# Per-column sums of the conditioning vectors: four transposes and four ScalarE copies with sums, where there were four products with a column of ones

## The reference, cut to what matters

```
c_act = silu(c)                               # one row of 1024
for i in range(4):
    mod = c_act @ ada_w[i] + ada_b[i]         # ada_w[i]: 1024 x 6144
    sh1, sc1, g1, sh2, sc2, g2 = split(mod, 6)
    h = modulate(rmsnorm(x, gain), sh1, sc1)  # h * (1 + sc1) + sh1
    x = x + g1 * mixer(h)                     # swa, gla, fox, swa in turn
    h = modulate(rmsnorm(x, gain), sh2, sc2)
    x = x + g2 * ((silu(h @ wg) * (h @ wu)) @ w_down)
```

## Time and profile before

| | |
|---|---|
| median of 3 runs | 2258.88 us (2257.32 to 2260.17) |
| the profiled execution's own time | 2258.98 us |
| its span, first to last instruction | 2257.2 us |
| mean granted PE clock | 0.989 |
| instructions | 33992 |
| DMA packets | 475.60 MB, mean 211 GB/s |

### The profile page before, as it was taken

One profiled execution on the slowest core, in us unless ns is written; L12 is line 12 of the kernel. 1 busy time (PEld: TensorE's weight loads), 2 busy tenths in 40 slices (PEclk: granted clock), 3 DMA queues, 4 the chain that ended last, 5 costly groups with the idle time before them and its releaser, 6 DMA issues.

```text
span 2257.2 us, 33992 instructions
## 1 busy us (share of the span) xinstructions
PE 2161.0 (96%) x13827; PEld 1925.4 (85%) x13827; DVE 1565.2 (69%) x2153; ACT 1029.4 (46%) x1698; POOL 186.2 (8%) x202
## 2 busy tenths in 40 slices
PE   6899999999999999989999999999999999999997
PEld 5799888888998888767999787899898899778996
DVE  5477757766777577566898677899745896657444
ACT  5344445544444455455444444433445434464333
POOL 1000001101000011011001001001000001111000
PEclk9999999999999999999999999999999999999999
DMA  8876745566766445623899534699643697525651
GB/s 281 285 227 229 254 156 165 172 224 225 240 232 233 157 160 173 229 98 126 283 342 346 180 119 143 223 350 356 220 145 131 236 353 242 177 85 177 201 188 66
DMA packets 297104, 475.60 MB, mean 211 GB/s; under 512 B 19936, under 2 KB 151466, under 8 KB 296948
## 3 DMA queue, kind: packets, MB, share of 16 engines
q1 hardware_dynamic: 286548, 440.67, 57.5%
q0 software_dynamic: 10400, 32.76, 4.8%
HBM read 465.88 MB, written 7.47 MB: 210 GB/s over the span
## 4 chain that ended last, share of the span: by engine, by line
PE 87%; DVE 6%; DMA 2%; ACT 2%; issue 2%; POOL 1%; SPq 0%; DVEq 0%; POOLq 0%; ACTq 0%
PE G L138 68%; PE A L138 16%; PE G L141 2%; DVE pool L158 1%; DMA raw<-in_w_in 1%; DVE wlo L150 1%; DVE pool L150 1%; ACT pool L144 1%; POOL sm L150 1%; PE A L141 1%; DVE X L150 1%; ACT HTh L144 0%; DVE sm L155 0%; DMA pool<-mod_rows 0%; DMA pool<-in_ada_b 0%
## 5 line engine op out<-in xcount | busy, mean ns | idle before, releaser
L150 DVE TENSOR_TENSOR wlo<-raw,whi 128x1024 fp32r<-128x1024 f32 x640 | 774.2, 1238 | 199.7 <-ACT whi L144 198.2
L144 ACT ACTIVATE whi<-raw 128x1024 fp32r<-128x1024 f32 x640 | 646.3, 1054 | 211.4 <-DMA raw<-in_ffn_w_gu 91.8
L138 PE MATMUL G<-HTh,whi 128*128 128x256 f32 x2336 | 671.9, 288 | 12.0 <-DVE wlo L150 7.0
L138 PE MATMUL G<-HTh,wlo 128*128 128x256 f32 x2336 | 661.6, 283 | 0.0
L138 PE MATMUL G<-HTl,whi 128*128 128x256 f32 x2336 | 661.5, 283 | 0.0
L138 PEld LDWEIGHTS G<-HTh,whi 128*128 128x128 f32 x2336 | 448.4, 192 | 19.6 <-DVE wlo L150 10.8
L138 PEld LDWEIGHTS G<-HTl,whi 128*128 128x128 f32 x2336 | 448.7, 192 | 2.1
L138 PEld LDWEIGHTS G<-HTh,wlo 128*128 128x128 f32 x2336 | 448.3, 192 | 0.0
L144 ACT ACTIVATE pool<-G 128x512 f32<-128x512 f32 (+2 forms) x208 | 115.4, 573 | 537.6 <-PE G L138 504.3
L138 PE MATMUL G<-whi,HTh 128*128 128x512 f32 (+1 forms) x784 | 314.7, 401 | 26.3 <-DVE wlo L150 14.4
L138 PE MATMUL G<-whi,HTl 128*128 128x512 f32 (+1 forms) x784 | 304.6, 389 | 4.5 <-DVE HTl L158 4.1
(11 more groups left out here) (196 smaller groups left out, 2241.1 us busy)
## 6 DMA issues: line engine op xcount, KB each, us to landing
raw<-in_ada_w SPq DMA_DIRECT2D x192, 512.0 KB, 5.9
raw<-in_ffn_w_gu SPq DMA_DIRECT2D x352, 256.0 KB, 4.9
raw<-in_w_in SPq DMA_DIRECT2D x128, 512.0 KB, 4.5
raw<-in_ffn_w_down SPq DMA_DIRECT2D x88, 512.0 KB, 6.6
raw<-in_w_in SPq DMA_DIRECT2D x160, 256.0 KB, 4.8
raw<-in_swa_w_in SPq DMA_DIRECT2D x24, 512.0 KB, 5.3
pool<-mod_rows POOLq DMA_DIRECT2D x24, 512.0 KB, 6.4
raw<-in_gla_w_in SPq DMA_DIRECT2D x24, 512.0 KB, 5.2
```

What stands on the lines that cost most here:

```text
L138: return self.e.matmul(out, a, b, start=start, stop=stop, skip_group_check=True) if self.e else self
L144: return self.e.activation(out, a, func, bias=bias, scale=scale, accum_out=accum) if self.e else self
L150: return self.e.tensor_tensor(out, a, b, op) if self.e else self
```

## The change

On PE the four products become four transposes of 128 x 128 into the same bank. ACT copies each of the four transposed blocks back over the accumulator, with a sum along the row (`accum`) into four columns `tot` of `sm`. DVE adds the bias to `tot` instead of to the bank. The ACT part is laid into `soon` with a count of 1 and DVE's with a count of 2. The bank is marked held until the ACT part is placed, is free for PE when ACT is done (before: DVE's add), and the accumulator's place in `pool` is released by ACT (before: by PE). A sum is only placed if two of the four `G` banks are not held (before: one). In the model of the clocks ACT is charged 1.8 us.

```diff
     def ada_sums(self, age=6):
-        while self.adaq and self.steps - self.adaq[0][4] >= age and not all(self.gheld):
+        while self.adaq and self.steps - self.adaq[0][4] >= age and self.gheld.count(False) > 1:
             l, u, b, acc, _ = self.adaq.pop(0)
             g = self.gbank()
             summed, m = ("pe_ada", (l, u)), ("ve_mod", (l, u))
-            self.h_ada_sum(g, b, acc, self.gfree[g], summed, l, u, m)
-            b.release([summed])
-            self.gfree[g] = [m]
-            if u == 11:
-                self.h_amod(l, m, ("ve_mod", (l, "a")))
-                self.modq.append(l)
+            self.h_ada_tr(g, b, acc, self.gfree[g], summed)
+            self.gheld[g] = True
+
+            tot, added = self.smc(4), ("ac_ada", (l, u))
+
+            def total(g=g, b=b, summed=summed, tot=tot, added=added):
+                self.spend("ACT", 1.8)
+                self.h_ada_sum(g, b, summed, added, tot)
+                b.release([added])
+                self.gfree[g], self.gheld[g], self.gage[g], self.bclk[g] = [added], False, max(self.gage) + 1, self.clk["ACT"]
+
+            def biased(l=l, u=u, tot=tot, added=added, m=m):
+                self.h_ada_mod(added, l, u, tot, m)
+                if u == 11:
+                    self.h_amod(l, m, ("ve_mod", (l, "a")))
+                    self.modq.append(l)
+            self.soon += [[1, total], [2, biased]]
...
         for n in range(4):
-            mm = e.matmul(M.GB[g][:, n:n + 1], b.a[:, n * P:n * P + P], M.ones[:, :], True, True)
+            mm = e.transpose(M.GB[g][:, n * P:n * P + P], b.a[:, n * P:n * P + P], M.ident[:, :])
...
+    def h_ada_sum(self, g, b, summed, added, tot):
+        e = self.e
+        e.wait_ge(*self.at(summed))
+        for n in range(4):
+            c = slice(n * P, n * P + P)
+            op = e.activation(b.a[:, c], self.M.GB[g][:, c], ACT.Copy, accum=tot[:, n:n + 1])
+        op.then_inc(*self.up(added))
...
-        e.tensor_tensor(M.mod[:, m:m + 4], M.GB[g][:, 0:4], M.adb[:, c:c + 4], ALU.add).then_inc(*self.up(done))
+        e.wait_ge(*self.at(added))
+        e.tensor_tensor(M.mod[:, m:m + 4], tot, M.adb[:, c:c + 4], ALU.add).then_inc(*self.up(done))
```

More of the change, by code:

```diff
@@ L456, in h_none @@
         pass
-    h_load = h_memset = h_piece = h_split = h_rest = h_ada = h_ada_sum = h_mm = h_mm1 = h_none
+    h_load = h_memset = h_piece = h_split = h_rest = h_ada = h_ada_tr = h_ada_sum = h_ada_mod = h_mm = h_mm1 = h_none
     h_copy = h_silu = h_tanh = h_gate = h_square = h_rstd = h_mean = h_pow = h_rows = h_none
@@ L2097, in h_mm1, with h_ada_tr @@
         mm.then_inc(*self.up(done))
-    def h_ada_sum(self, g, b, acc, free, summed, l, u, done):
+    def h_ada_tr(self, g, b, acc, free, summed):
         e, M = self.e, self.M
@@ L2103, in h_ada_sum @@
         e.wait_ge(*self.at(acc))
-        e.wait_ge(*self.at(self.tconst))
+        e.wait_ge(*self.at(self.tid))
         for n in range(4):
-            mm = e.matmul(M.GB[g][:, n:n + 1], b.a[:, n * P:n * P + P], M.ones[:, :], True, True)
+            mm = e.transpose(M.GB[g][:, n * P:n * P + P], b.a[:, n * P:n * P + P], M.ident[:, :])
         mm.then_inc(*self.up(summed))
@@ L2724, in h_ada, with h_ada_mod @@
             op.then_inc(*self.up(done if c else ("ve_ada", (done[1], 0))))
-    def h_ada_sum(self, g, b, acc, free, summed, l, u, done):
+    def h_ada_mod(self, added, l, u, tot, done):
         e, M = self.e, self.M
-        e.wait_ge(*self.at(summed))
         e.wait_ge(*self.at(self.tadb))
         m, c = l * 64 + u * 4, l * 48 + u * 4
-        e.tensor_tensor(M.mod[:, m:m + 4], M.GB[g][:, 0:4], M.adb[:, c:c + 4], ALU.add).then_inc(*self.up(done))
+        e.wait_ge(*self.at(added))
+        e.tensor_tensor(M.mod[:, m:m + 4], tot, M.adb[:, c:c + 4], ALU.add).then_inc(*self.up(done))
     def h_silu(self, out, ps, full, free, tanh, done):
```

## The result

The changed kernel takes 2293.65 us (median of 4 runs, 2291.92 to 2295.9) against 2258.78 for the kernel before, measured beside it: a ratio of 1.0155, with a 95% interval of 1.014 to 1.0169. It is 35 us slower where 19.5 us less were forecast.

A forecast was written before the change was run, and what follows sets the result against it. PE, busy for 96% of the span, was taken to bound the kernel. From 2258.98 us, 7.4 + 11.0 + 0.6 + 2.5 − 2.0 = 19.5 us less gave 2239.5, stated as 2239; its own range was 2231 to 2246, the overall range 2231 to 2252.

The forecast's parts named there:

- Bounds for the 16 sums: Mixer layers: ACT's 1.4 us before softmax copies and `OTh` costs between 0 and 22 us; 2 taken.
- 7.4 + 2.5 − 2.0: Mixer layers: 7.4 us saved on PE at 16 sums, 2.5 of PE's 4.6 us waits gone, 2 lost to ACT.
- The fourth rival: Attention order recorded anew, PE's waits change by chance: a few microseconds either sign, inside the range, no chance of its own.
- The second rival: PE waits for ACT at attention copies and splits, up to 1.4 us a sum: 2259 to 2304; slower 0.05.
- the feed-forward cushion: First two feed-forward stretches: no piece has under 6.0 us from `wlo` to its matmuls, so new 0.5 us stalls fit.
- The transposes: PE at each of 48 sums: four transposes take 0.44 us against 0.90 now, saving 0.46 each, 22.1 in all.
- the third rival: PE pays each transpose's record, 0.27 us, so four cost 1.1 against 0.90: 10 us slower, 2269; chance 0.03.
- The two long feed-forward stretches: First two feed-forward stretches, 24 sums: PE's saving counts in full, 11.0 us.
- the first rival: Two long feed-forward stretches give nothing, with DMA share at 0.99 to 1.00: 2250 us; chance 0.20.
- The third stretch: Third feed-forward stretch: 3.7 us saved on PE, only 0.6 counted; PE waits for `wlo` as DVE has no time over.
- the stall removed: Mixer layers: bias addition a step later removes most of PE's 4.6 us waits behind DVE's `mod`; half taken, 2.5.
- ACT's copies: ACT at each sum: four copies at 0.36 us, 1.4 us a sum, 69 us in all; ACT has room.

The follow-up runs named there:

- the order alone: Changed kernel's order on every engine, with charge, held bank and deferral, but the old products and no ACT copies: 2294.18 us, 1.0156 to the kernel before.

## Why the prediction was wrong

**The step that failed** is the sentence that bounds ACT's effect in the mixer layers: "Bounds for the 16 sums are 0 (ACT otherwise idle, or the clocks of `advance` place the rest around the 1.8 us charged) and 16 times 1.4, 22 us", from which I took 2 us. Together the mixer layers were to gain 7.9 us (7.4 + 2.5 − 2.0); alone (the change in them only) they cost 45. I read the charge as something that lets the planner protect PE. It does the opposite: a modelled ACT clock that runs ahead stops `advance` from recording splits, and they fall behind the next instruction that waits for PE. That is shown by the charge alone in the kernel before (+38 us), by its removal (−49), and by the splits put first with the charge in place (−45.6). The bound was also wrong in kind: part of the waits are at evacuations with no sum near, so the number of sums times the length of a sum bounds nothing.

**The fourth rival** said "the order of the attention is recorded anew with other clocks" and gave it "a few microseconds of either sign", without a case of its own. It was this one, with 36 us for the order alone, 20 of waits and 13 of slower products in the profiled execution. I had printed how PE's order differs in the two mixer layers and never followed one changed place of ACT to the PE wait that it makes.

**The second rival** had the right sign and mostly the wrong mechanism. It needed ACT's 1.4 us to be exposed, and the feed-forward cushion used up. ACT's time is exposed in part (the copies at 229.67 are 1.0 of a wait of 3.44), but waits of 3.4 us for `wlo` come without any copies, and the feed-forward parts lost none of what they were to gain.

**What held.** The transposes: 0.44 us forecast and read, so the third rival falls. The Trainium skill's figure ("TensorE: Matmul & The Clock Gate", Part 4), whose data are bf16 where these are f32, fits the duration of a record, 0.27 us (0.60 for four, less three steps of 0.11), and not what a transpose costs in this stream, 0.11. The two long feed-forward stretches: −11.0 forecast, −11.1 read between the waits; the first rival falls. One reading there was off: in the second stretch of before a piece at 1470.46 has 5.2 us of cushion, not 6.0. Of the cushion much was used: the smallest of the same pieces are 3.9 and 3.4 us in the changed kernel. The third stretch: −0.6 forecast, −0.5 measured, in part by luck. The 0.6 was the cushion of one piece, while the sums of the same paragraph leave DVE 8.13 less 7.69, 0.44 us a sum, 3.5 in all; and PE waited for the gated product `pool<-pool,G`, not for `wlo`. DVE's idle time ahead of `mod` fell from 61.9 us to 15.4. DVE's addition a step later was worth more than I gave it: 2.5 us for the stall removed, where what it avoids is 28.6.

**What was mis-sized.** ACT's copies: 1.4 us a sum forecast from the exponentials of the earlier trace rows, 1.0 measured, 48 us of ACT in all, not 69. The mixer layers, even with no charge: I forecast 7.4 + 2.5 − 2.0 = 7.9 us, and at piece 260 that kernel is 3.2 ahead. It has its own new waits there, 2.34 us for `pool` until 174.20, where the kernel before has 0.63, and 1.19 for `S` until 274.02. My total of 19.5 less would have been 15 without the charge.

**Open:** why a charge of 1.0 costs less than 0.5 or 1.8. That the slower products come from the lower clock is read from the traces; waits and clock were not tried apart.

## What to carry over

A planner's charge is an edit of the program: compare the recorded order of each in-order engine at each place that moved, and ask of every instruction that moved behind a wait who needs its result next. An instruction that prepares the next product should stand ahead of the one that waits for the end of this product, even where a cost model says that its engine is busy. When work moves to another engine, move the instruction that uses its result later too: the kernel without the charge, 2244 us, beats both kernels here, and with the addition at once it is slower than the kernel before.

## What was unexpected of the hardware

A pause of PE costs more than its length. After 3.44 us of waiting, until 233.07, the records went from 0.28 to 0.41 us and the steps from 0.12 to 0.21, until 236.5. From 233.4 to 236.6 us the granted clock was 0.50, which is the level of 1.2 GHz, and from 237 to 243 it was 1.00, the level of 2.4 GHz. Over 216 to 264 us it was 0.79 in the mean, where it had been 1.00 in the same layer of before. The four copies with a sum took 0.25 us each from start to start, though the record of one is 0.28 and each is followed by a read of the accumulator (0.19 us at 229.84): the records overlap.
